# The clearing of the experts' gate table in DRAM is made to wait for TensorE

## The chip, the cores and the metric

One core of one Trainium2 chip runs the whole program in one launch. The metric is the device time of the program in microseconds (us): the median of the runs shown.

## The reference, cut to what matters

The program computes two transformer blocks on 256 tokens of width 2048. The first block has multi-head latent attention (MLA, 8 heads) and sliding-window attention side by side, then a layer that picks 16 of 16384 experts per head for each token. Here is the part of the MLA whose inputs are prepared when the change takes effect, and the sparse expert layer whose gates are kept in DRAM:

```python
q = (rms_norm(q_lat, q_a_gain) @ w_q_b).reshape(B, S, MLA_HEADS, MLA_QK)
kv = (rms_norm(kv_lat, kv_a_gain) @ w_kv_b).reshape(B, S, MLA_HEADS, MLA_NOPE + MLA_V)
k = jnp.concatenate([k_nope, broadcast(k_pe)], axis=-1)       # k_pe is shared by the 8 heads
q, k = rms_norm(q, q_gain), rms_norm(k, k_gain)                # then rope on the last 64 of each
s = einsum('bqhd,bkhd->bhqk', q, k) * scale                    # causal softmax, times v
...
w = gc * gelu(xc @ expert_u[ic])                               # gc: the gates of the chosen experts
y = w @ expert_v[ic]
```

The kernel evaluates all 16384 experts densely and multiplies them by a table of gates, `scr_g`, of 16384 experts by 256 tokens in float32 (16.8 MB in DRAM), which is zero where an expert is not chosen.

## The kernel before, in words

One Python function, `walk`, goes through the whole program once for each engine. It calls `go(step, ...)`, which emits the step if the engine at hand has it, and `up(engine, name)` or `landing(name)`, which count the semaphore that the step raises. `latest[engine]` is the last such mark of an engine in the order of the walk. `fresh(engine, marks)` turns marks into the waits that this engine still needs. Each engine executes its own list strictly in the order of the walk. Work beside the matrix products is written as generators in the list `tasks`; each call of `step()` moves every task on by one `yield`, so that transposes, splits and square sums are woven between weight pieces.

Weights come as 512 KB pieces through SyncE's DMA queue into five buffers `raw` (`load_piece`, line 2748). ScalarE rounds a piece into `whi` (line 1872), VectorE makes the rest `wlo` (line 2102), TensorE multiplies both (line 1649, twelve matmuls of 512 columns for a piece). Activations are transposed by TensorE four 128x128 blocks at a time (line 1723, semaphore `transposed`) and split into high and low parts by ScalarE and VectorE (lines 1857, 1887, 2145, 2148).

The stretch in question is the first 170 us: 43 pieces (`w_in_a`, `w_in_b`, `w_kv_b`, `w_q_b`), ending with `queries(1)`, the last product of the latent queries. During it `k_rope` spreads the shared rotary key over the heads in two passes of one buffer, `prows`: GpSimd zeroes the buffer (`zero`, memset at line 2680), VectorE writes the scaled key into half of it (`spread_kpe`, line 2355), TensorE transposes it, and the second pass begins when the buffer is free again. The MLA scores (`mla_scores`, line 1649) need all eight key splits, and so both passes. VectorE's list holds the `spread_kpe` of the second pass ahead of the last splits of the latent queries.

Right after `queries(1)` the walk reaches this code:

```python
lend_banks()
go("gate_blank")
t_blank = up("POOL", "gate_blank")
for c in range(8):
    go("gate_clear", c, fresh("POOL", t_blank))
    t_clear = landing("gate_cleared")
while len(qt_done) < 6 or len(kt_done) < 8 or not t_rq:
    step()
```

`gate_blank` (line 2688) zeroes 128x256 words of SBUF with GpSimd; `gate_clear` (line 2694) is a DMA from GpSimd's queue that writes them 16 times, 2 MB of `scr_g`; there are eight. At that point of the walk GpSimd's list holds, in order: the constants, five small loads, the `zero` of the sliding-window keys, the `zero` of the first `k_rope` pass, `gate_blank`, the eight clears, the `zero` of the second `k_rope` pass (it comes from a `step()` of the loop above), then the reload of `x` (line 2685), and from 515 us on the scatters into the table (line 2699), which wait for the clears' landing. TensorE's latest mark at `go("gate_blank")`, followed through the walk, is the 24th of the semaphore `transposed`: the `step()` behind the last piece of `queries(1)` has already put one more group of four transposes behind it.

Of the kernel before, what the change touches and what calls it, by code (L numbers as in the profile page):

```python
# [37 lines left out]
def build(nc, D, out):  # L38
# [12 lines left out]
    with ExitStack() as ctx:  # L51
# [5 lines left out]
        def sem(name):  # L57
            if name not in sems:
                sems[name] = ctx.enter_context(nc.semaphore(name))
            return sems[name]  # L60
# [138 lines left out]
        def walk(steps):  # L199

            count, latest, passed = {}, {}, {}

            def go(step, *a):
                if step in steps:
                    steps[step](*a)

            def up(engine, name):
                count[name] = count.get(name, 0) + 1
                latest[engine] = (sem(name), count[name])
                return latest[engine]  # L210
# [88 lines left out]
            def lend_banks():  # L299
                for _ in range(2):  # L300
                    pair, free = take(accs)
                    misc.give(2 * pair, free)
                    misc.give(2 * pair + 1, free)
# [619 lines left out]
            tasks.append(q_scale())  # L923
            tasks.append(pairs_freed())
            lend_banks()
            go("gate_blank")
            t_blank = up("POOL", "gate_blank")
            for c in range(8):
                go("gate_clear", c, fresh("POOL", t_blank))
# [717 lines left out]
        def tensor_program(e):  # L1647
# [192 lines left out]
            def na_pv(bank, pt, h, ready):  # L1840
                for mark in ready:
                    e.wait_ge(*mark)
                for t in range(2):
# [4 lines left out]
                last.then_inc(sem("weighed"), 1)  # L1848

            walk({"consts": consts, "mm": gemm_piece, "mm_rows": gemm_rows, "mm_wide": wide_piece, "transpose": transpose, "bias_mm": bias_mm,  # L1850
                  "kpe_mm": kpe_mm, "kpe_turn": kpe_turn, "swa_scores": swa_scores, "swa_pv": swa_pv,
                  "mla_scores": mla_scores, "mla_pv": mla_pv, "sub_scores": sub_scores,
                  "da_scores": da_scores, "da_pv": da_pv, "na_scores": na_scores, "na_pv": na_pv})

        def scalar_program(e):
# [190 lines left out]
            def square_hi(zi, k, ready):  # L2046
                for mark in ready:
                    e.wait_ge(*mark)
                act(BH[:, k:k + 2, :], zs[zi].rearrange("p (m n) -> p m n", m=2), ACT.Copy, "square_hi")

            walk({"prime": prime, "consts": consts, "split": split, "x_square": x_square, "x_split": x_split, "row_squares": row_squares,
                  "group_squares": group_squares, "head_square": head_square, "evac2": evac2, "row_exp": row_exp,
                  "sink_exp": sink_exp, "copy_pt_a": copy_pt, "rope_tables": rope_tables, "scaled_cols": scaled_cols,
# [7 lines left out]
        def vector_program(e):  # L2061
# [581 lines left out]
            def down_add(b, c, ready):  # L2643
                for mark in ready:
                    e.wait_ge(*mark)
                for t in range(2):
                    last = e.tensor_tensor(Y[:, t, c], Y[:, t, c], b[t][:, :], ALU.add)
                last.then_inc(sem("down_add"), 1)

            walk({"consts": consts, "split": split, "x_square": x_square, "norm_stat": norm_stat, "norm_part": norm_part, "norm_row": norm_row, "row_squares": row_squares,  # L2650
                  "x_split": x_split, "head_sum": head_sum, "head_root": head_root, "head_scale": head_scale, "rope": rope, "evac2": evac2,
                  "row_max": row_max, "biased_max": biased_max, "sink_gap": sink_gap, "row_inv": row_inv, "copy_pt_v": copy_pt, "above": above, "above_sel": above_sel, "table_steps": table_steps,
# [13 lines left out]
        def gpsimd_program(e):  # L2666
            def prime(s):
                e.memset(s, 1.0).then_inc(sem("prime"), 1)

            def load_inputs(BD):  # L2670
                e.dma_start(GC[:, :], D["gain_cols"]).then_inc(sem("gain_cols_landed"), 16)
                e.dma_start(POS[:, :], D["pos"]).then_inc(sem("pos_landed"), 16)
                e.dma_start(C[:, 834:882], D["consts"][:, 834:882]).then_inc(sem("freq_landed"), 16)
                e.dma_start(GR[:, :], D["gain_rows"]).then_inc(sem("gain_rows_landed"), 16)
                e.dma_start(BD, D["table"]).then_inc(sem("table_landed"), 16)

            def zero(ts, ready):
                for mark in ready:
                    e.wait_ge(*mark)
                e.memset(ts, 0.0).then_inc(sem("zeroed"), 1)  # L2680

            def reload_x(ready):
                for mark in ready:
                    e.wait_ge(*mark)
                e.dma_start(R[:, :, :], x_v).then_inc(sem("x_again"), 16)

            def gate_blank():
                e.memset(blank, 0.0).then_inc(sem("gate_blank"), 1)

            def gate_clear(c, ready):  # L2690
                for mark in ready:
                    e.wait_ge(*mark)
                rows = D["scr_g"].rearrange("(c p r) t -> c p r t", c=8, p=128)
                e.dma_start(rows[c], blank.unsqueeze(1).to_broadcast([128, 16, 256])).then_inc(sem("gate_cleared"), 16)

            def gate_scatter(t, k, ready):
                for mark in ready:
                    e.wait_ge(*mark)
                e.indirect_dma_start(out=D["scr_g"].rearrange("e (t o) -> (e t) o", o=1),  # L2699
                                     out_offset=bass.IndirectOffsetOnAxis(ap=EID[t][:, k:k + 1], axis=0),  # L2700
                                     in_=GT[t][:, k:k + 1], in_offset=None, compute_op=ALU.add
                                     ).then_inc(sem(f"gate_scattered{t}"), 16)

            def fetch(sc, ready):
                i = sc % 2
                for mark in ready:
                    e.wait_ge(*mark)
                e.dma_start(glt[i], D["scr_a"][sc, :, :]).then_inc(sem(f"gelu_fetched{i}"), 16)  # L2708
                e.dma_start(gtt[i].rearrange("p (k t) -> p k t", k=8),
                            D["scr_g"][1024 * sc:1024 * sc + 1024, :].rearrange("(k p) t -> p k t", p=128)  # L2710
                            ).then_inc(sem(f"gate_fetched{i}"), 16)

            def load_lam(ready):
                for mark in ready:
                    e.wait_ge(*mark)
                e.dma_start(lamb, D["lam"]).then_inc(sem("lam_landed"), 16)

            def na_bias(h, ready):
                for mark in ready:
                    e.wait_ge(*mark)  # L2720
                e.dma_start(nbs[h % 2], D["na_bias"][h, :, :]).then_inc(sem(f"na_bias_landed{h % 2}"), 16)

            def load_post(name, ready):
                for mark in ready:
                    e.wait_ge(*mark)
                e.dma_start(grow, D[name].partition_broadcast(128)).then_inc(sem("post_landed"), 16)

            walk({"prime": prime, "load_inputs": load_inputs, "zero": zero, "reload_x": reload_x,
                  "gate_blank": gate_blank, "gate_clear": gate_clear, "gate_scatter": gate_scatter,
                  "fetch": fetch, "load_lam": load_lam,  # L2730
                  "na_bias": na_bias, "load_post": load_post})
# [163 lines left out]
```

## Time and profile before

| | |
|---|---|
| median of 3 runs | 3259.15 us (3258.58 to 3262.24) |
| the profiled execution | 3259.14 us, span 3257.3 us |
| TensorE busy in the span | 3200.2 us, 98% |
| VectorE, ScalarE, GpSimd busy | 65%, 47%, 15% |
| chain that ended last | TensorE 90%, VectorE 6% |
| granted TensorE clock, mean | 0.99 |

Read it from the top: TensorE is busy nearly throughout, so any stretch in which it stands still shows at the end. Times in the rows below are counted from the span's start.

### The profile page before, as it was taken

The numbers are of one execution on the slowest core, as the hardware profiler recorded it, in microseconds if no ns is written. First come the engines' busy times: TensorE is split into PE (matmuls) and PEld (weight loads), VectorE is DVE, ScalarE is ACT, GpSimd is POOL, SyncE is SP. The second block draws the span as 40 slices with busy tenths as digits, with TensorE's granted clock in tenths as the row PEclk, the third lists the DMA queues.
The fourth block names the chain that finished last, engine by engine and source line by source line (L and its number), as shares of the span: only waits on it lengthen the run. The fifth ranks groups of instructions, "written<-read, shape, count | busy, mean of one in ns | idle before, by whom it ended". The sixth has DMA issues, their size and how long they took to land.

```text
span 3257.3 us, 40800 instructions
## 1 busy us (share of the span) xinstructions
PE 3200.2 (98%) x16112; PEld 2715.7 (83%) x16112; DVE 2106.2 (65%) x3062; ACT 1517.7 (47%) x2006; POOL 492.0 (15%) x322
## 2 busy tenths in 40 slices
PE   8989999999999999999999999999999999999998
PEld 7788888888888888888888888888888788888886
DVE  6766578887555576666666565565465655655556
ACT  5645454545444444444444544445444544444443
POOL 1000005777777200000000000000000000000000
PEclk9999999999999999999999999999999999999999
DMA  8623557888888866666665555444555455555554
GB/s 321 252 85 130 181 183 208 214 214 215 212 214 211 262 249 244 250 248 245 245 233 200 197 184 174 165 170 176 191 194 188 174 192 191 193 189 193 189 192 149
DMA packets 220286, 660.95 MB, mean 203 GB/s; under 512 B 56704, under 2 KB 56848, under 8 KB 217536
## 3 DMA queue, kind: packets, MB, share of 16 engines
q1 hardware_dynamic: 170864, 600.81, 52.9%
q0 software_dynamic: 49232, 57.54, 8.7%
q8 instruction: 127, 2.08, 0.3%
q14 instruction: 63, 0.52, 0.0%
HBM read 622.48 MB, written 35.78 MB: 202 GB/s over the span
## 4 chain that ended last, share of the span: by engine, by line
PE 90%; DVE 6%; ACT 2%; issue 1%; DMA 1%; DVEq 0%; ACTq 0%; SPq 0%
PE PS L1649 89%; DVE wlo L2102 2%; PE PS L1723 2%; ACT whi L1872 1%; DMA raw<-in_w_in_b 0%; DVE R L2606 0%; ACT M L1914 0%; DVE AA L2148 0%; ACT Y L1958 0%; DVE TMP L2177 0%; DVE M L2507 0%; DVE TMP L2178 0%; DVE BB L2148 0%; DMA R<-in_x 0%; DMA M<-in_na_bias 0%
## 5 line engine op out<-in xcount | busy, mean ns | idle before, releaser
L2102 DVE TENSOR_TENSOR wlo<-raw,whi 128x1024 fp32r<-128x1024 f32 x1101 | 1343.8, 1224 | 889.6 <-ACT whi L1872 878.4
L1872 ACT ACTIVATE whi<-raw 128x1024 fp32r<-128x1024 f32 x1101 | 1157.8, 1057 | 1033.4 <-PE PS L1649 998.3
L1649 PE MATMUL PS<-whi,AA 128*128 128x512 f32 (+1 forms) x2880 | 718.7, 390 | 2.0 <-DVE AA L2148 1.2
L1649 PE MATMUL PS<-whi,BB 128*128 128x512 f32 x2640 | 667.4, 393 | 1.7 <-DVE wlo L2102 1.2
L1649 PEld LDWEIGHTS PS<-whi,AA 128*128 128x128 f32 x2880 | 537.0, 189 | 112.4 <-DVE AA L2148 2.0
L1649 PE MATMUL PS<-BB,whi 128*128 128x512 f32 x2304 | 577.4, 392 | 1.7 <-DVE BB L2148 1.7
L1649 PEld LDWEIGHTS PS<-whi,BB 128*128 128x128 f32 x2640 | 491.1, 188 | 102.3 <-DVE wlo L2102 1.8
L2699 POOL DMA_INDIRECT scr_g<-M x256 | 446.9, 1746 | 426.4 <-issue 390.2
L1649 PEld LDWEIGHTS PS<-BB,whi 128*128 128x128 f32 x2304 | 414.4, 189 | 76.1 <-DVE BB L2148 1.9
L1649 PE MATMUL PS<-wlo,AA 128*128 128x512 f32 (+1 forms) x1440 | 389.4, 388 | 1.9 <-DVE wlo L2102 1.9
L1649 PE MATMUL PS<-wlo,BB 128*128 128x512 f32 x1320 | 356.3, 389 | 0.5 <-DVE wlo L2102 0.5
L1649 PEld LDWEIGHTS PS<-BB,wlo 128*128 128x128 f32 x2304 | 314.3, 190 | 22.5
L1649 PE MATMUL PS<-BB,wlo 128*128 128x256 f32 x2304 | 321.2, 282 | 0.0
L1649 PEld LDWEIGHTS PS<-wlo,AA 128*128 128x128 f32 x1440 | 271.2, 188 | 58.0 <-DVE wlo L2102 2.3
L1649 PEld LDWEIGHTS PS<-wlo,BB 128*128 128x128 f32 x1320 | 247.7, 188 | 53.1 <-DVE wlo L2102 0.9
L1649 PE MATMUL PS<-AA,whi 128*128 128x512 f32 (+1 forms) x1056 | 263.8, 391 | 2.6 <-DVE AA L2148 2.2
L1649 PEld LDWEIGHTS PS<-AA,whi 128*128 128x128 f32 (+1 forms) x1056 | 189.4, 188 | 37.2 <-DVE AA L2148 2.8
L1649 PEld LDWEIGHTS PS<-AA,wlo 128*128 128x128 f32 (+1 forms) x1040 | 141.8, 189 | 10.0
L1649 PE MATMUL PS<-AA,wlo 128*128 128x256 f32 (+1 forms) x1040 | 147.2, 282 | 0.0
L1857 ACT ACTIVATE AA<-M 128x512 fp32r<-128x512 f32 x72 | 45.5, 632 | 150.8 <-DVE M L2507 143.8
L1857 ACT ACTIVATE M<-TMP 128x512 f32<-128x512 f32 x64 | 40.5, 633 | 128.1 <-DVE TMP L2498 100.5
L2708 POOL DMA_DIRECT2D M<-scr_a x16 | 8.8, 547 | 589.8 <-DVE AA L2514 543.6
(236 smaller groups left out, 1570.0 us busy)
## 6 DMA issues: line engine op xcount, KB each, us to landing
raw<-in_peer_u SPq DMA_DIRECT2D x256, 512.0 KB
raw<-in_peer_v SPq DMA_DIRECT2D x256, 512.0 KB
raw<-in_w_in SPq DMA_DIRECT2D x160, 512.0 KB
raw<-in_w_up SPq DMA_DIRECT2D x128, 512.0 KB
raw<-in_w_down SPq DMA_DIRECT2D x128, 512.0 KB
raw<-in_w_out SPq DMA_DIRECT2D x64, 512.0 KB
raw<-in_w_in_a SPq DMA_DIRECT2D x32, 512.0 KB
scr_g<-M POOLq DMA_DIRECT2D x8, 2048.0 KB, 30.1
```

The source lines that it names most:

```text
L1649: return e.matmul(outp, l, r, start=start, stop=stop)
L1723: last = e.transpose(banks[bank][:, 128 * n:128 * n + 128], s, ident)
L1857: e.activation(o, x, func, **kw).then_inc(sem(name), 1)
L1872: e.activation(whi[:, n % NH, :], raw[:, n % NR, :], ACT.Copy).then_inc(s_hi, 1)
L2102: e.tensor_tensor(wlo[:, n % NH, :], raw[:, n % NR, :], bf(whi[:, n % NH, :]), ALU.subtract).then_inc(s_lo, 1)
L2699: e.indirect_dma_start(out=D["scr_g"].rearrange("e (t o) -> (e t) o", o=1), out_offset=bass.IndirectOffsetOnAxis(ap=EID[t][:, k:k + 1], ax ...
L2708: e.dma_start(glt[i], D["scr_a"][sc, :, :]).then_inc(sem(f"gelu_fetched{i}"), 16)
```

## The change

`gate_blank` gets a list of waits, and the walk gives it TensorE's latest mark. Nothing else is changed: the same instructions in the same order on every engine.

```diff
             lend_banks()
-            go("gate_blank")
+            go("gate_blank", fresh("POOL", latest["PE"]))
             t_blank = up("POOL", "gate_blank")
             for c in range(8):
                 go("gate_clear", c, fresh("POOL", t_blank))
...
-            def gate_blank():
+            def gate_blank(ready):
+                for mark in ready:
+                    e.wait_ge(*mark)
                 e.memset(blank, 0.0).then_inc(sem("gate_blank"), 1)
```

## Rows read from the trace of the kernel before

**Rows 1.** The page: the span, and the chain that ended last by engine.

```profile
span 3257.3 us, 40800 instructions
PE 90%; DVE 6%; ACT 2%; issue 1%; DMA 1%; DVEq 0%; ACTq 0%; SPq 0%
```

**Rows 2.** GpSimd's timeline: start, duration, instruction, idle time before and its releaser.

```profile
3.57 0.54 POOL L2675 DMA_DIRECT2D ST<-in_table  x1
37.54 0.95 POOL L2680 MEMSET R<- 128x1024 f32 x1 [33.43 <-PE PS L1649]
38.43 0.95 POOL L2680 MEMSET M<- 128x1024 f32 x1
39.33 0.31 POOL L2688 MEMSET M<- 128x256 f32 x1
39.93 8.00 POOL L2694 DMA_DIRECT2D scr_g<-M  x7 [0.30 <-POOL M L2688]
105.00 1.12 POOL L2694 DMA_DIRECT2D scr_g<-M  x1 [57.07 <-issue]
154.68 0.95 POOL L2680 MEMSET M<- 128x1024 f32 x1 [48.56 <-PE PS L1723]
212.57 0.73 POOL L2685 DMA_DIRECT2D R<-in_x  x1 [56.95 <-DVE AA L2148]
```

**Rows 3.** The table's instructions: clears one and two, clears six and seven, clear eight.

```profile
L2694 POOL DMA_DIRECT2D scr_g<-M x2: 1137/1189/1241, 39.9 to 41.0; - x2
DMA to landing us min/median/max: 10.0/13.6/17.1
...
L2694 POOL DMA_DIRECT2D scr_g<-M x2: 1666/1720/1773, 45.1 to 46.2; - x2
DMA to landing us min/median/max: 51.4/54.9/58.4
...
L2694 POOL DMA_DIRECT2D scr_g<-M x1: 1122/1122/1122, 105.0 to 105.0; - x1
DMA to landing us min/median/max: 12.2/12.2/12.2
```

**Rows 4.** The chain that ended last, 153 to 167 us: start, duration, what.

```profile
153.56 0.34 DVE M L2182
...
156.29 0.68 DVE M L2355 x2
157.02 2.83 PE PS L1723 x12
...
164.59 2.36 DVE AA L2148 x6
167.00 1.01 PE PS L1649 x3
```

**Rows 5.** TensorE's timeline from the last piece to the first scores.

```profile
149.57 1.07 PE L1649 MATMUL PS<-wlo,BB 128*128 128x512 f32 x4
153.96 0.66 PE L1723 MATMUL PS<-C,M 128*128 128x128 f32 x4 [3.32 <-DVE M L2182]
157.02 5.78 PE L1723 MATMUL PS<-C,M 128*128 128x128 f32 x28 [2.40 <-DVE M L2355]
167.00 1.01 PE L1649 MATMUL PS<-BB,AA 128*128 128x256 f32 x3 [4.20 <-DVE AA L2148]
```

**Rows 6.** Stretches: length, busy (count) of PE, PEld, DVE, ACT, POOL; clock, DMA share, GB/s.

```profile
39.00:150.00 111.00, 105.77 (x510) 85.60 (x509) 84.74 (x173) 64.16 (x153) 9.75 (x10) 1.00 0.82 309
...
44.00:50.00 6.00, 4.41 (x22) 3.31 (x20) 5.76 (x10) 2.85 (x5) 3.93 (x4) 1.00 1.02 390
50.00:54.00 4.00, 3.73 (x16) 3.10 (x17) 4.00 (x8) 2.73 (x6) 0.00 (x0) 1.00 1.02 332
54.00:56.50 2.50, 2.50 (x12) 2.07 (x12) 2.36 (x8) 1.06 (x1) 0.00 (x0) 1.00 0.97 252
70.00:100.00 30.00, 29.27 (x133) 23.75 (x132) 17.92 (x42) 15.82 (x30) 0.00 (x0) 1.00 1.02 413
...
157.00:167.00 10.00, 5.78 (x28) 5.55 (x29) 7.73 (x23) 6.50 (x21) 0.00 (x0) 0.67 0.03 11
167.00:173.00 6.00, 6.00 (x31) 6.00 (x31) 0.00 (x0) 0.00 (x0) 0.00 (x0) 0.55 0.01 3
160.00:197.00 37.00, 32.80 (x258) 32.56 (x256) 21.67 (x50) 15.12 (x45) 0.00 (x0) 0.88 0.00 1
```

**Rows 7.** DMA queues in 50 to 54 us: packets, MB, share of 16 engines.

```profile
q0 software_dynamic: 324, 1.33, 102.2%
```

**Rows 8.** VectorE's timeline while the first seven clears are issued.

```profile
42.26 1.12 DVE L2279 TENSOR_SCALAR TMP<-TMP 128x64 f32<-128x64 f32 x1
43.42 3.77 DVE L2281 TENSOR_SCALAR TMP<-TMP 128x64 f32<-128x64 f32 x1
47.23 1.00 DVE L2291 SCALAR_TENSOR_TENSOR TMP<-TMP 128x64 f32<-128x64 f32 x4
48.26 0.20 DVE L2294 TENSOR_SCALAR TMP<-TMP 128x64 f32<-128x64 f32 x1
49.00 1.22 DVE L2102 TENSOR_TENSOR wlo<-raw,whi 128x1024 fp32r<-128x1024 f32 x1
```

**Rows 9.** TensorE's and ScalarE's timelines, 46 to 63 us.

```profile
50.27 1.20 PE L1649 MATMUL PS<-wlo,AA 128*128 128x512 f32 x4 [1.86 <-DVE wlo L2102]
62.71 0.33 PE L1649 MATMUL PS<-AA,whi 128*64 128x256 f32 x1 [0.34 <-DVE wlo L2102]
...
60.33 1.06 ACT L1872 ACTIVATE whi<-raw 128x1024 fp32r<-128x1024 f32 x1 [4.96 <-DMA raw<-in_w_in_b]
```

**Rows 10.** SyncE's queue after the last piece that it can load ahead.

```profile
151.97 0.43 SPq L2753 DMA_DIRECT2D R<-in_key_pos  x1
152.44 0.43 SPq L2753 DMA_DIRECT2D TMP<-in_key_pos  x1
197.88 0.33 SPq L2753 DMA_DIRECT2D R<-in_key_pos  x1
```

**Rows 11.** The whole trace, the table's instructions: the scatters.

```profile
L2699 POOL DMA_INDIRECT scr_g<-M x256: 1544/1547/2580, 515.0 to 1085.0; - x128
```

## The prediction

> **What bounds the kernel.** I read the page first: the chain that ended last is TensorE for 90% of the span [rows 1], so a change matters if it makes TensorE stand still or lets it go on sooner. Then, because the diff touches only GpSimd, I read GpSimd's timeline [rows 2]. The reader is to see three things in it. The clears are issued at 39.93 us, long before the walk's place for them, since GpSimd's list has nothing else to do. Seven are issued in a row in 8.00 us, and the eighth only at 105.00 us, after 57.07 us in which nothing that the profile shows held it. And behind the eighth, in the same list, stands the memset of the second pass of `k_rope` at 154.68 us. Next the landings of the clears [rows 3], then the chain around 155 us and TensorE's timeline there [rows 4, 5], the DMA rates by stretch [rows 6, 7], and last what VectorE and TensorE did while the clears were issued [rows 8, 9].
>
> **What the change does to GpSimd's list.** It adds one wait. The mark is TensorE's 24th `transposed`; the group of four transposes that raises it runs at 153.96 us [rows 5] and ends about 0.65 us later. The memset that now runs at 154.68 us was released by TensorE's transposes too [rows 2], so 154.68 us is also when the new wait ends. Everything in the list from `gate_blank` on moves there: one memset of 0.31 us, eight DMA issues, and behind them the memset of 0.95 us for `prows`. On its side VectorE waits with line 2355 for that memset, and TensorE's 28 transposes at 157.02 us wait for line 2355 [rows 4, 5]. VectorE's list is in order, so the splits of the latent queries behind line 2355 wait too, and the first scores at 167.00 us wait for the last of these splits. Nothing can fill the hole: TensorE's own list goes on with those transposes.
>
> **When the eighth clear is issued.** The seventh is issued at about 46.2 us and lands 58.4 us later, at 104.6 us; the sixth lands at 45.1 + 51.4 = 96.5 us; the eighth is issued at 105.00 us [rows 2, 3]. So the eighth did not start when one of its forerunners was through, nor when six were, but 0.4 us after the seventh. I take this as the queue's behaviour: seven clears of 2 MB fit, the eighth waits until they are all through. The list ahead of them is the same after the change, so the same seven should fit.
>
> The Trainium skill, page "DMA: Bandwidth & Descriptors", section "SWDGE vs HWDGE vs iDMA", has GpSimd append one pair of descriptors per DMA operation to rings in a carveout of SBUF. Taken literally, the eighth would start as soon as the first has freed its places; the rows show a wait for the seventh. What the literal reading would give stands among the rivals.
>
> **How long seven clears take with the engines to themselves.** After 160 us the DMA engines are idle until 197 us [rows 6], and the two loads of `key_pos` issued at 152 us [rows 10] are over by the time that the first clear's packets can start, so the clears run alone. The first one lands 10.0 us after its issue; in the trace it had the engines nearly to itself too. For the other six I need a rate of clears alone. In 50 to 54 us only GpSimd's queue moved anything (324 packets, 102.2% of the engines [rows 7]), at 332 GB/s [rows 6]. The bounds are 413 GB/s (70 to 100 us, clears and weights mixed) and 252 GB/s (54 to 56.5 us, the slowest stretch under load); 390 GB/s in 44 to 50 us is the start of the burst and lies between. I take 332, the one row in which clears run alone and steadily: 2.097 MB / 332 GB/s = 6.32 us each, 37.9 us for six (30.5 at 413, 49.9 at 252).
>
> The same page's section "Bandwidth" lists 425 GB/s for a 16 MB load into SBUF. By an estimate from that figure six clears would take 29.6 us and the sum below would come to about 3298 us; the clears are stores, and the row that has them alone is slower.
>
> **The sum.** First issue: 154.68 + 0.60 (39.33 to 39.93 in [rows 2]) = 155.28. Seventh landed: + 10.0 + 37.9 = 203.2. Eighth issued: + 0.4 = 203.6. Its issue takes 1.1, the memset 0.95, VectorE's start 0.05: 205.7. Line 2355 started at about 156.2 before. So TensorE's first scores come 49.5 us later (42.1 and 61.5 at the bounds of the rate). The chain between line 2355 and the scores (10.8 us, [rows 4]) has the same members as before, so it moves as a whole.
>
> **Does the clock add to it?** TensorE's granted clock is 0.67 in 157 to 167 us and 0.55 in 167 to 173 us, after idle pieces of 3.32, 2.40 and 4.20 us [rows 5, 6]: the scores begin at its lower level, 1.2 GHz, already in the kernel before. A longer hole cannot lower it further; the price of getting back is in the trace as it stands. I cost it at nothing.
>
> **What the change takes away.** Between 39 and 115 us the clears no longer compete. Two things can be seen. VectorE's operations of 64 columns on `TMP` took 1.12 and 3.77 us while GpSimd issued the clears, and 0.20 to 0.25 us each right after the last issue of the seven [rows 8]. They held up the split at 49.00 us, for which TensorE waited 1.86 us [rows 9]. And the piece `w_in_b` arrived 4.96 us late for ScalarE, of which TensorE lost 0.34 us [rows 9]; five buffers covered the rest. Together 2.2 us. The floor is 0 (the gain is lost in later waits on VectorE). The ceiling is all of TensorE's idle time in the 111 us from 39 to 150 us: 111.00 - 105.77 = 5.2 us [rows 6].
>
> **What else moves.** The clears land by about 210 us. Their first reader is the scatter at 515.0 us [rows 11], so the later landing is free. The reload of `x` at 212.57 us [rows 2] waits for VectorE's work after the attention and moves with it. SyncE's next load at 197.88 us [rows 10] moves likewise, to about 247 us, where the clears are over.
>
> Net: 49.5 - 2.2 = +47.3 us. The profiled execution took 3259.14 us against a median of 3259.15 us, so the same sum holds for both: 3259.1 + 47.3 = 3306.4 us, about 1.5% slower.
>
> **Rivals.** (a) The queue takes the eighth as soon as there is room for it, so after the first clear's landing. Eighth issued at 155.28 + 10.0 + 0.4 = 165.7, memset over at 167.7: 11.6 us late, less 2.2, gives 3268.5 us. For it: nothing in this kernel demands that a full queue be emptied. Against it: in the trace six landings passed without releasing the eighth [rows 3].
>
> (b) The wait of 57.07 us came from the competition with the weights, and with free engines the eighth follows the seventh. GpSimd still needs 8.00 + 1.1 us for its issues before the memset: 9.2 us late, less 2.2, gives 3266.1 us. Against it: the admission came 0.4 us after a landing, in the midst of unchanged traffic.
>
> (c) On the other side, no slower than before: the clears cost more than other issues only because the engines are full (1.12 to 1.77 us each against 0.54 us for the small loads [rows 2, 3]). With eight issues of 0.54 us and no block the memset would be 4.3 us late, less 2.2: 3261 us, within what can be told. It decides from a delay of 8.7 us downwards (6.5 us of resolution plus 2.2 us of relief). Against it: the first clear met empty engines and still took 1.14 us.
>
> (d) That the change does nothing, because the mark is passed early: excluded by the mark's own time, 153.96 us against 39.33 us.
>
> **How the numbers follow.** Chances: 0.83 for the full drain, 0.07 for (a), 0.04 for (b), 0.03 for (c), 0.03 for anything else. The prediction is the likeliest case's, 3306 us. Its range takes the bounds of the two uncertain terms: 42.1 - 5.2 gives 3296.0 at the low end, 61.5 - 0 gives 3320.6 at the high end. Since no more than 0.17 lies outside the case, its range is the range: 3296 to 3321. A measurement of this kernel can tell about 0.2% (6.5 us) from no change. Slower by more than that: the drain, (a), half of (b) and a part of the rest, 0.93. Within it: (c) and the other half of (b), 0.06. Faster: 0.01.
>
> **What the profile after would show.** Step by step: `gate_blank` released by TensorE's transposes at about 152.5 us; seven issues in 8 us; the eighth about 48 us after the first, 0.4 us behind the landing of the seventh; the memset of line 2680 right behind it, at about 202 us, and line 2355 waiting for it; TensorE idle for about 50 us in one piece ahead of the 28 transposes, which now wait for GpSimd through line 2355; line 2281 back at 0.2 us and no wait of 1.86 us near 48 us. The prediction is wrong if the eighth clear is issued well ahead of the seventh's landing, if the clears alone run far from 332 GB/s, or if the idle piece is given back somewhere before 300 us.

## The result, and the profile after

The changed kernel takes 3303.85 us (median of 4 runs, 3303.6 to 3304.56) against 3258.86 us for the kernel before (4 runs): a ratio of 1.0139, 95% interval 1.0123 to 1.0155, or 45.0 us more. The forecast was 3306 us, 47.3 us more.

The page of the changed kernel, its span and its chain by engine (against [rows 1]):

```profile
span 3302.0 us, 40800 instructions
PE 89%; DVE 6%; issue 2%; ACT 2%; DMA 0%; POOL 0%; DVEq 0%; ACTq 0%; SPq 0%
```

There are as many instructions as before. GpSimd's timeline, with the same columns as in [rows 2]:

```profile
36.05 0.95 POOL L2680 MEMSET R<- 128x1024 f32 x1 [31.96 <-PE PS L1649]
...
150.92 0.31 POOL L2690 MEMSET M<- 128x256 f32 x1 [113.03 <-PE PS L1723]
151.53 7.98 POOL L2696 DMA_DIRECT2D scr_g<-M  x7 [0.30 <-POOL M L2690]
200.05 1.12 POOL L2696 DMA_DIRECT2D scr_g<-M  x1 [40.54 <-issue]
201.09 1.04 POOL L2680 MEMSET M<- 128x1024 f32 x1
258.12 0.72 POOL L2685 DMA_DIRECT2D R<-in_x  x1 [55.99 <-DVE AA L2148]
```

The blank and seven clears start when TensorE raises the mark. The eighth stands for 40.54 us with no releaser, and right behind it comes the memset that stood free at 154.68 us before. The clears' landings (the table's instructions that are under way in 157 to 159 us, which are the fifth, sixth and seventh; against [rows 3]):

```profile
L2696 POOL DMA_DIRECT2D scr_g<-M x3: 1556/1663/1768, 155.7 to 157.7; - x3
DMA to landing us min/median/max: 32.0/37.3/41.8
```

The seventh is issued at 157.7 us and lands 41.8 us later, at 199.5 us; the eighth follows at 200.05 us. Who waited for the memset, in VectorE's timeline:

```profile
202.16 0.76 DVE L2355 TENSOR_TENSOR M<-M,ST 128x256 f32<-128x256 f32 x2 [50.08 <-POOL M L2680]
```

And who waited for VectorE, in TensorE's timeline (against [rows 5]):

```profile
149.75 1.11 PE L1723 MATMUL PS<-C,M 128*128 128x128 f32 x4 [3.32 <-DVE M L2182]
202.98 5.34 PE L1723 MATMUL PS<-C,M 128*128 128x128 f32 x28 [52.12 <-DVE M L2355]
212.97 1.01 PE L1649 MATMUL PS<-BB,AA 128*128 128x256 f32 x3 [4.64 <-DVE AA L2148]
```

TensorE's one long hole is named after line 2355 on VectorE, but VectorE had itself stood for 50.08 us; the reader has to go one step further, to GpSimd, and there past the memset to the issue in front of it. By stretches (against [rows 6]):

```profile
155.00:195.00 40.00, 0.00 (x0) 0.00 (x0) 0.00 (x0) 0.00 (x0) 4.51 (x4) 0.50 1.01 330
...
213.00:219.00 6.00, 6.00 (x34) 6.00 (x35) 0.00 (x0) 0.00 (x0) 0.00 (x0) 0.63 0.01 3
219.00:226.00 7.00, 7.00 (x62) 7.00 (x61) 4.11 (x7) 5.02 (x17) 0.00 (x0) 1.00 0.00 1
```

For 40 us no compute engine but GpSimd is busy, and the DMA engines are full with the clears alone, at 330 GB/s; GpSimd's queue is the only one that moves anything (155 to 195 us, with the columns of [rows 7]):

```profile
q0 software_dynamic: 3319, 13.20, 100.7%
```

The granted clock is 0.50 in the hole, its lower level. In the first 6 us of the scores it is 0.63 and then 1.00; before it was 0.55 ([rows 6]) and then 1.00 (173 to 180 us). So the longer hole left the scores no slower a start.

**Where the 44.7 us between the two profiles come from.** Four distances give the sum. To the first memset of line 2680, before any clear is issued: 36.05 against 37.54 us, -1.5 us; this start differs from profile to profile (35.6 to 37.6 us over all of this study). From there to the mark: 114.87 against 117.14 us, -2.3 us. From the mark to the first scores: 62.05 against 12.32 us, +49.7 us. From the scores to the end: 3089.0 against 3090.3 us, -1.3 us. Sum +44.7 us (-1.49 - 2.27 + 49.73 - 1.27).

Two runs of one kernel can differ by more than the first and the last of these: 25 runs of the kernel before span 3255.94 to 3261.56 us.

### The profile page after: what moved, and what is told of

The parts are those of the page before. It is cut to its first block, busy times and chain, and to the rows that moved or that the text cites. A ratio compares the mean times of both kernels' runs of the same rounds, so it can differ in the third digit from the quotient of the medians.

```text
span 3302.0 us, 40800 instructions
## 1 busy us (share of the span) xinstructions
PE 3196.1 (97%) x16112; PEld 2712.9 (82%) x16112; DVE 2100.3 (64%) x3062; ACT 1516.9 (46%) x2006; POOL 492.8 (15%) x322
## 4 chain that ended last, share of the span: by engine, by line
PE 89%; DVE 6%; issue 2%; ACT 2%; DMA 0%; POOL 0%; DVEq 0%; ACTq 0%; SPq 0%
PE PS L1649 87%; DVE wlo L2102 2%; PE PS L1723 2%; ACT whi L1872 1%; ACT M L1914 0%; POOL scr_g L2696 0%; DVE R L2606 0%; DMA M<-in_na_bias 0%; DVE AA L2148 0%; DVE M L2211 0%; ACT Y L1958 0%; DVE TMP L2177 0%; DVE M L2507 0%; DVE TMP L2178 0%; DVE BB L2148 0%
## 5 line engine op out<-in xcount | busy, mean ns | idle before, releaser
L1723 PE MATMUL PS<-C,M 128*128 128x128 f32 x284 | 45.6, 288 | 66.5 <-DVE M L2355 52.5
L1723 PEld LDWEIGHTS PS<-C,M 128*128 128x128 f32 x284 | 35.7, 148 | 77.7 <-DVE M L2355 53.3
```

Source lines behind the costliest of these rows:

```text
L1723: last = e.transpose(banks[bank][:, 128 * n:128 * n + 128], s, ident)
```

## The experiments

All are compared with the kernel before on the same chip. Its median there was 3258.58 us for the runs with the memset first, one early clear, half-size clears and the earlier piece, and 3258.61 us for the others. Code is shown against the changed kernel, and a ratio is to the kernel before.

### The same wait, but the memset goes first

```diff
+            t_lat_used = latest["PE"]
+            while len(qt_done) < 6 or len(kt_done) < 8 or not t_rq:
+                step()
-            go("gate_blank", fresh("POOL", latest["PE"]))
+            go("gate_blank", fresh("POOL", t_lat_used))
...
                 t_clear = landing("gate_cleared")
-            while len(qt_done) < 6 or len(kt_done) < 8 or not t_rq:
-                step()
```

> The clears wait for the same mark as in the change, but stand behind the second memset of line 2680 in GpSimd's list. If the loss is the list (the memset queued behind the blocked eighth clear), TensorE's hole of 52 us before the 28 transposes is gone, the clears still run alone from about 156 us on with the eighth about 48 us after the first, and the time is that of before less the relief of the first 150 us: 3254 to 3258 us. If the clears' traffic or their descriptors themselves hold up the preparation of the attention, the scores still start much later than 167 us and the time stays above 3270 us. In between: if issuing clears slows VectorE's splits at 157 to 165 us as it slowed its small operations at 41 to 47 us, a few us of the relief are lost (3258 to 3263 us).

Measured: 3263.92 us, ratio 1.0014 (1.0005 to 1.0024). Of the change's 45 us only 5.3 are left. GpSimd's timeline of this kernel (its lines are numbered one higher):

```profile
152.05 0.95 POOL L2681 MEMSET M<- 128x1024 f32 x1 [112.60 <-PE PS L1724]
152.95 0.30 POOL L2691 MEMSET M<- 128x256 f32 x1
153.55 7.98 POOL L2697 DMA_DIRECT2D scr_g<-M  x7 [0.30 <-POOL M L2691]
204.97 1.12 POOL L2697 DMA_DIRECT2D scr_g<-M  x1 [43.44 <-issue]
```

The eighth clear stands as long as in the change, and nobody waits behind it. So some 40 of the 45 us come from the order of the list and not from the clears' traffic. But the relief did not come through either (the time lies above even the 3258 to 3263 us of the third case), and its profile says why. VectorE's timeline:

```profile
159.32 1.46 DVE L2078 TENSOR_SCALAR RT<-ST 128x16 f32<-128x16 f32 x1
160.81 0.72 DVE L2082 TENSOR_SCALAR ST<-RT 128x16 int32<-128x16 int32 x1
...
204.69 1.28 DVE L2251 SCALAR_TENSOR_TENSOR Y<-POS,C,R 128x1024 f32<-128x1024 int32 x1 [3.38 <-DMA R<-in_key_pos]
```

TensorE's timeline:

```profile
166.21 1.01 PE L1650 MATMUL PS<-BB,AA 128*128 128x256 f32 x3 [6.36 <-DVE AA L2149]
...
206.03 6.51 PE L1650 MATMUL PS<-ST,Y 128*128 128x64 f32 x32 [3.82 <-DVE Y L2251]
```

And a stretch of it, with the columns of [rows 6]:

```profile
210.00:220.00 10.00, 10.00 (x45) 8.97 (x46) 5.19 (x9) 3.68 (x6) 0.72 (x1) 0.65 0.48 143
```

Two tiny VectorE operations took 1.46 and 0.72 us while clears were being issued (the same two take 0.17 us each in the changed kernel, at 207.90 and 208.11 us), and from the mark to the scores it was 14.16 us against 12.32. A load of `key_pos`, which was issued amid the clears' traffic, came 3.38 us late and held TensorE for 3.82 us. And behind this wait the granted clock was 0.65 for the stretch at 210 to 220 us; the kernel before was granted 1.00 in 206 to 216 us, at about the same work, and there the 32 matmuls of 64 columns took 4.00 us (204.47 and 206.87 us) in place of 6.51. So the clears do have a price of their own at this place: 8.2 us against the kernel with late clears below (3263.92 - 3255.68), not the 45 us of the change.

### One clear early, seven behind the mark

```diff
-            go("gate_blank", fresh("POOL", latest["PE"]))
+            go("gate_blank", [])
...
-                go("gate_clear", c, fresh("POOL", t_blank))
+                go("gate_clear", c, fresh("POOL", t_blank, latest["PE"] if c else None))
```

> The first clear runs unguarded at 39 us as before, the other seven wait for the mark. If seven clears fit the queue and an eighth waits for all to land, there is no block: the memset of line 2680 comes only some 8 us of issues late, and the time is about 3259 + 8 - 3 = 3264 us. If the loss came from the amount of clearing after the mark (14.7 of 16.8 MB are left), the time stays near 3298 to 3304 us.

Measured: 3298.66 us, ratio 1.0121 (1.0106 to 1.0136). The expectation of 3264 us was wrong, and with it the theory that seven may be outstanding. GpSimd's timeline:

```profile
39.37 1.14 POOL L2696 DMA_DIRECT2D scr_g<-M  x1 [0.30 <-POOL M L2690]
152.01 6.82 POOL L2696 DMA_DIRECT2D scr_g<-M  x6 [111.51 <-PE PS L1723]
193.97 1.12 POOL L2696 DMA_DIRECT2D scr_g<-M  x1 [35.15 <-issue]
195.01 1.04 POOL L2680 MEMSET M<- 128x1024 f32 x1
```

The first clear was through 100 us before, only six were outstanding, and still the eighth of the program stood, until those six were down (the last lands at 157.2 + 36.3 = 193.5 us). So what brings an issue to a stand is how much has been put into the list since the program began, and not how much is outstanding. The time alone would also fit the other case, a loss by the amount of clearing left after the mark; that one is ruled out by the run with the memset first, in which all 16.8 MB are left and 5.3 us are lost.

### Clears of half and of a quarter of the size

```diff
-            for c in range(8):
+            for c in range(16):
...
-                rows = D["scr_g"].rearrange("(c p r) t -> c p r t", c=8, p=128)
-                e.dma_start(rows[c], blank.unsqueeze(1).to_broadcast([128, 16, 256])).then_inc(sem("gate_cleared"), 16)
+                rows = D["scr_g"].rearrange("(c p r) t -> c p r t", c=16, p=128)
+                e.dma_start(rows[c], blank.unsqueeze(1).to_broadcast([128, 8, 256])).then_inc(sem("gate_cleared"), 16)
```

> As the change, but sixteen clears of 1 MB in place of eight of 2 MB. If the queue's limit is the amount of work in it (rows of 1 KB: seven times 2048 fit, eight times do not), fourteen are issued in a row (about 16 us) and the fifteenth waits; the memset is as late as in the change, or earlier by as much as the drain releases sooner: 3295 to 3306 us. If the limit is a count of seven transfers, the eighth waits for the first seven to land (7.3 MB, 24 us after the first issue), and issues after it wait again.

> As the change with 32 clears of 0.5 MB. A clear of 2 MB puts 128 rows of 1 KB on each of 16 engines, and a completion; 7 of 8 and 15 of 16 (of 64 rows) went through before the drain. With a list of 1024 places, of which the five small loads took 45, the sums are 45 + 7 x 129 = 948 and 45 + 15 x 65 = 1020, and of clears with 32 rows and a completion 29 should fit (1002) and the thirtieth wait. Were the limit 15 MB of data, thirty would fit. The time is near 3310 us in either case.

Measured: 3308.65 us with sixteen (ratio 1.0153, 1.0138 to 1.0169), and 3312.25 us with thirty-two (32 and `[128, 4, 256]` in the diff; one run). GpSimd's timelines, first of the one, then of the other:

```profile
151.75 13.09 POOL L2696 DMA_DIRECT2D scr_g<-M  x15 [0.30 <-POOL M L2690]
204.00 0.85 POOL L2696 DMA_DIRECT2D scr_g<-M  x1 [39.16 <-issue]
204.77 1.04 POOL L2680 MEMSET M<- 128x1024 f32 x1
```

```profile
152.72 22.96 POOL L2696 DMA_DIRECT2D scr_g<-M  x31 [0.30 <-POOL M L2690]
206.67 0.71 POOL L2696 DMA_DIRECT2D scr_g<-M  x1 [30.99 <-issue]
207.30 1.04 POOL L2680 MEMSET M<- 128x1024 f32 x1
```

Both are slower than the 3295 to 3306 us that I expected of sixteen, and than the 3310 us of thirty-two. Fifteen and thirty-one go through, and each time it is the one that would complete the 16.8 MB that stands. A count of seven transfers is refuted; so is my expectation of fourteen, and so is my estimate of 29, which added a completion for each transfer and the five small loads to 1024 places. In rows of 1 KB, shared evenly among the 16 DMA engines, 7 x 128 = 896, 15 x 64 = 960 and 31 x 32 = 992 pass and 1024 does not. That is as near as these runs come to the place. Every row here has 1 KB, so whether rows or bytes count stays open. Smaller pieces made it a little worse, since all but one now precede the drain (52.25 us from the first issue to the last in the one, 53.95 in the other, 48.52 in the change) and nothing is gained by admission in smaller steps.

In all these kernels the clear that stands is also the last one, so by themselves they can't tell a place in the list from something peculiar to the last clear. The scatters that follow in the same queue can. GpSimd's timeline of the kernel before, the 61st, 125th and 189th of the 256 scatters (the 253rd has 4.01 us):

```profile
659.42 1.54 POOL L2699 DMA_INDIRECT scr_g<-M  x1 [4.28 <-issue]
...
806.34 1.54 POOL L2699 DMA_INDIRECT scr_g<-M  x1 [2.76 <-issue]
...
945.90 1.54 POOL L2699 DMA_INDIRECT scr_g<-M  x1 [4.62 <-issue]
```

The program has no wait at these four (its waits are at the 1st, 17th, 33rd and so on); the other scatters without a wait follow their neighbours after 0.30 or 0.31 us. In all ten profiles it is these same four, 64 apart, whether the clears were 8, 16 or 32. So the standing comes back at a fixed distance in the list, and the number of transfers has not moved it: a transfer does not take a place of its own that these runs could see.

### Six and seven clears early

```diff
-            go("gate_blank", fresh("POOL", latest["PE"]))
+            go("gate_blank", [])
...
-                go("gate_clear", c, fresh("POOL", t_blank))
+                go("gate_clear", c, fresh("POOL", t_blank, latest["PE"] if c >= 6 else None))
```

> Six clears run unguarded at 39 us as before, the last two wait for the mark. The run with one early clear showed that the eighth of the program waits however long the first is through, so the theory is now: at a certain place of the descriptors' list, which the eighth reaches, the queue is drained before it goes on. Then the eighth waits for the seventh alone, which the mark has released: 10 us to land, 0.5, the eighth's issue and the memset, about 13 us late and little relief, so 3268 to 3272 us. If what matters were how much is outstanding at the eighth (seven fit), nothing would wait here and the memset would be 3 us late: 3259 to 3262 us.

> Seven clears run unguarded at 39 us, only the eighth waits for the mark. Drain theory: all seven have landed at 105 us, so the eighth has nothing to wait for, the memset is about 1.1 us late, and the time is that of before within 2 us (3257 to 3261 us). A theory in which the eighth has a cost of its own at its place (a fixed wait) gives more than 3265 us.

Measured: 3267.69 us with six early (ratio 1.0029, 1.0018 to 1.0039), and 3259.36 us with seven early (`c >= 7`; ratio 1.0002, 0.9992 to 1.0011). GpSimd's timelines:

```profile
153.13 1.11 POOL L2696 DMA_DIRECT2D scr_g<-M  x1 [107.33 <-PE PS L1723]
162.45 1.12 POOL L2696 DMA_DIRECT2D scr_g<-M  x1 [8.21 <-issue]
163.49 1.04 POOL L2680 MEMSET M<- 128x1024 f32 x1
```

```profile
155.41 1.12 POOL L2696 DMA_DIRECT2D scr_g<-M  x1 [108.98 <-PE PS L1723]
156.45 1.04 POOL L2680 MEMSET M<- 128x1024 f32 x1
```

With one transfer outstanding the eighth stands for 8.21 us, for one landing (the seventh lands at 153.1 + 8.8 = 161.9 us); with none it does not stand at all. The first time is 0.3 us below the 3268 to 3272 us that the drain theory gave, the second inside its 3257 to 3261 us. Together with the change and the run of one early clear this makes a series: seven, six, one and none outstanding at the eighth give 40.54, 35.15, 8.21 and 0 us of standing, and 45, 40, 9 and 1 us of time. In the nine profiles in which something is outstanding, the clear that stood is issued 0.4 to 0.7 us after the last landing. At its place in the list the queue is drained of whatever is in it.

### The clears behind an earlier piece, and much later

The first waits for TensorE's use of the piece `w_in_b` (63 us); the second puts two clears ahead of each of the first four products of the expert queries.

```diff
-            last = used_up()
+            last = t_pe_used = used_up()
...
-            go("gate_blank", fresh("POOL", latest["PE"]))
+            go("gate_blank", fresh("POOL", t_pe_used))
```

> The clears wait for TensorE's use of the piece w_in_b (about 68 us) instead of the last latent queries' piece. The eighth is then admitted some 55 to 60 us later, at about 125 us, well ahead of the memset at 154 us, so the list's theory gives no loss: the time of before less the relief of the stalls near 48 and 62 us, 3255 to 3258 us. A theory in which any delay of the clears costs time would give more than before.

```diff
-            go("gate_blank", fresh("POOL", latest["PE"]))
-            t_blank = up("POOL", "gate_blank")
-            for c in range(8):
-                go("gate_clear", c, fresh("POOL", t_blank))
-                t_clear = landing("gate_cleared")
...
             for u in range(8):
+                if u == 0:
+                    go("gate_blank", fresh("POOL", latest["PE"]))
+                    t_blank = up("POOL", "gate_blank")
+                if u < 4:
+                    for c in (2 * u, 2 * u + 1):
+                        go("gate_clear", c, fresh("POOL", t_blank, latest["PE"]))
+                        t_clear = landing("gate_cleared")
                 gemm_wide("peer_w_q", [u], BB, nP, q_post, LEADT)
```

> No clear before the expert queries: two ahead of each of the first four products of peer_w_q (from about 320 us on), behind TensorE's latest mark, and nothing behind them in GpSimd's list but the scatters from 515 us on. The first 215 us then hold neither the clears' traffic, nor their descriptors, nor a blocked list: 3254 to 3257 us, 2 to 5 us less than before. If the clears' cost merely moves (VectorE or the weights slowed at 320 to 420 us), it is that of before.

Measured: 3257.38 us for the earlier piece, ratio 0.9998 (0.9989 to 1.0007), the same as before; 3255.68 us for the late pairs, ratio 0.9991 (0.9982 to 1.0000), 2.9 us less, at the edge of what can be told. In the first the eighth clear went out at 129.29 us, ahead of the memset, so a delay by itself costs nothing. But its relief was gone again: from the first memset to the mark it took 116.84 us against 117.14 before. It issues its clears at 64 to 72 us, and there VectorE's timeline has

```profile
69.83 1.78 DVE L2077 TENSOR_SCALAR RT<-ST 128x4 f32<-128x4 f32 x1
71.64 0.72 DVE L2081 TENSOR_SCALAR ST<-RT 128x4 int32<-128x4 int32 x1
72.40 0.16 DVE L2085 TENSOR_TENSOR RT<-ST 128x4 f32<-128x4 f32 x1
```

on the way to the key columns, for which TensorE then waited 2.9 us (0.7 us before). In the second the same distance is 114.42 us, and the eighth clear stands for 31.88 us at 373 to 405 us with only the scatters of 511 us behind it (its lines are numbered two higher):

```profile
371.89 1.11 POOL L2698 DMA_DIRECT2D scr_g<-M  x1 [8.92 <-PE PS L1651]
404.88 1.12 POOL L2698 DMA_DIRECT2D scr_g<-M  x1 [31.88 <-issue]
510.99 1.84 POOL L2703 DMA_INDIRECT scr_g<-M  x1 [104.99 <-DVE M L2481]
```

## Why the prediction was right, and which step of it was not

- **The mark and the list.** As forecast: released by TensorE's 24th group of transposes, seven issues in 7.98 us, the memset behind the eighth, line 2355 waiting for it. Putting the memset first removes the hole; that shows the cause.
- **When the eighth is issued.** The time was right (0.5 us behind the seventh's landing, forecast 0.4), the reason wrong. I wrote that seven clears of 2 MB fit and the eighth waits until they are all through. The runs with one, six and seven early clears, and with smaller ones, show a place in the list, counted from the start of the program, at which the queue is drained of what is outstanding. In this change the two say the same, since all eight stand behind the mark; for the run with one early clear they differ by 35 us (3264 us forecast, 3298.66 us measured), and there the first theory failed. That a wrong reading gave the right time here was luck.
- **How long seven clears take.** 9.3 us for the first (10.0 taken over from before) and 38.7 us for the other six (37.9 at 332 GB/s). Alone they ran at 330 GB/s. The choice of the one row in which clears ran alone decided this: at the 413 GB/s of mixed traffic the sum would have come out 7.4 us lower.
- **The sum to the scores.** 49.5 us forecast, 49.7 us measured. The clock added nothing, as argued.
- **What the change takes away.** 2.2 us forecast, 2.3 us between the two profiles. The waits of 1.86 and 0.34 us are gone, and line 2281 takes 0.20 us in place of 3.77. In the profiles in which no clear is issued before the mark, the distance from the first memset to the mark is 114.4 to 114.9 us; with six to eight early it is 116.6 to 119.4 us. So the size rests on a spread of about its own width.
- **What was left over.** The measured difference is 45.0 us, 2.3 us less than forecast. In the two profiles 1.5 us of that lie before the first clear, where the change can't act, and 1.3 us behind the scores. Runs of one kernel spread by more than that, so nothing is explained by them.
- **The rivals.** That room for one is enough (3268.5 us) is refuted by the standing of 40.54 us, and again by the run with one early clear. That the standing came from competition with the weights (3266 us) falls with it: between 155 and 195 us nothing but the clears moved. The cheap issue (3261 us) too: an issue took 1.14 to 1.77 us with no traffic beside the clears' own.

## What to carry to other kernels

Before a wait is put in front of a group of DMA issues, read what stands behind them in the same engine's list, and how long the issues themselves stood in the trace: a gap in an issuing engine with no releaser costs nothing only as long as nothing behind it is due, and a wait moves that gap to a new place. Large background transfers from GpSimd are best put where its list is empty behind them and where VectorE has no chain of tiny operations to run; here the late place took 2.9 us off, at the edge of what can be told, and the wrong place cost 45.

## What the runs showed of the hardware that had not been expected

- GpSimd's DMA queue stands at a place of its list until all its outstanding transfers have landed, even one transfer (8.21 us) and even if the earlier ones are long through. The place is reached between 992 and 1024 rows of 1 KB for each DMA engine, if they share evenly. It comes back in the scatters, at the 61st and every 64th after it, for 2.8 to 4.6 us each in the kernel before.
- Clears of 2 MB from SBUF to DRAM run at 330 GB/s alone; mixed with weight loads in the other direction the engines moved 413 GB/s ([rows 6]), and 390 GB/s over 340 to 410 us of the run with late pairs.
- While GpSimd issues large transfers, VectorE's tiny `TENSOR_SCALAR` operations take 0.7 to 3.8 us in place of 0.16 to 0.20 us, at 41 to 47, 70 to 72 and 159 to 161 us in three kernels, each time exactly where the issues are; `TENSOR_TENSOR` splits of 1024 columns beside them stay at 1.23 us (68.69 us in the run with the earlier piece). It does not hit each of them: beside the issue of the eighth clear at 105.00 us in the kernel before, one at 105.09 us took 0.18 us. The Trainium skill, page "SBUF — State Buffer", section "SBUF: two separate sides", describes one pair of ports that VectorE in certain modes and GpSimd take by an exclusive lock, whoever comes first. What the page works out is GpSimd held up by VectorE; these rows are in keeping with the lock in the other direction. In which mode these operations ran no row shows.
